# One sparse expert moved to the end of a mixture-of-experts stage, and two weight transfers moved ahead of the first gather

## Chip, cores, metric

One core of a Trainium2 chip runs the whole layer. The metric is device time in microseconds (us) from start to end of one execution; the figure quoted is the median over the runs. TensorE, VectorE, ScalarE, GpSimd and SyncE are called PE, DVE, ACT, POOL and SP, as in the profile.

## The reference

One layer on 512 tokens of width 1024, float32. A mixer (differential attention and a Mamba-2 scan, both projected from one matrix) adds to the residual, then a mixture of experts, then a gated per-layer embedding, then a norm. What matters here is the experts:

```
h = rms_norm(x)
logits = h @ router_w + router_b               # 512 x 32
top_vals, top_idx = top_k(logits, 4); gate = softmax(top_vals)
for each token and each of its 4 experts e:
    gu = h @ w_up[e] + b_up[e]                 # 1024 -> 2048
    g, u = min(gu[:1024], 7), clip(gu[1024:], -7, 7)
    y += gate * (((u + 1) * g * sigmoid(1.702 g)) @ w_down[e] + b_down[e])
x = x + y
```

There are 512 x 4 = 2048 rows of work for 32 experts, 64 each on average. The weights of one expert are 8 MiB (`w_up`) and 4 MiB (`w_down`).

## The kernel before

All engines run hand-written programs joined by semaphores. Until about 780 us they compute the mixer. From there on:

**Routing.** PE does the output projection tile by tile (`out_proj`, 4 tiles of 128 tokens), DVE adds it to the residual `xs` (`add_out`, L1745) and normalizes it (`normalize`, L1345), ACT writes the normalized rows to `h2_dram` (`store_h2`, L1103). PE turns each tile, ACT copies the turned tile to `h_tile` (two buffers, `evacuate`, L1105), and PE multiplies it with the router (`route`, L2324). `h_tile` lies in the bytes that the first pair of rows of `w_up` will hold, so SP may load that pair only when all four tiles are routed. DVE picks the top four (`choose`, L1721), clears the bias tiles (memset, L1754), ranks the tokens of each expert, and builds the slot tables. `slot_token` (L1826) says which token fills which slot of which expert. It waits for all of `h2_dram` (L1824). Then DVE sorts experts by size (L1828 to L1857) and writes their order to `control`; `rows_u` (L1868) closes the tables, with `tables_ready` at 3.

**Rounds.** Each expert is a round `b` of 96 slots (`CAP`), or of 64 (`PAIR`) if it is one of the `SMALLS` = 14 experts with the fewest tokens. Round 0, 1 and 2 are large, then 14 pairs of a small and a large round follow (`pair`, L2558), and the last round, 31, is always expert 31, with 96 slots. If any expert doesn't fit, `extra` is positive and all engines run `AGAIN` = 35 further rounds. In a round POOL gathers the tokens (`fetch`, L729), PE turns them (`turn_x`, L2413), DVE copies them to `x_T` (`copy_x`, L1873), PE multiplies with `w_up` (`up`, L2432, or `up_small`, L2453), ACT and DVE form the activation (`swish`, `take_u`, `join`), PE turns it (`turn_act`, L2421), ACT copies it (`copy_act`, L1165), and PE multiplies with `w_down` (`down`, `down_small`). PE's order is `up(b)`, `turn_x(b+1)`, `down(b-1)`, `turn_act(b)`. ACT stores the rows to `y_dram` (`expert_out`, L1144).

**Weights.** `w_up` and `w_down` have one buffer each, in four pairs of row blocks (2 MiB and 1 MiB per pair). SP loads pair `c` of the next expert when PE has used it: `up_used`, `down_used` (L555, L569). All matmuls carry L2026 and all transfers of `w_up` and `w_down` carry L556 and L570.

**End.** The last round's rows are not stored. `down_last` (L2526) leaves them in PSUM, and PE spreads them over the tokens with a 0/1 matrix (`hot_last`, L1891, `turn_last_slots`, `sum_last`). The other rows come from `y_dram` by 16 indirect gathers on POOL (`gather_rows`, L759), which DVE adds up (`gather`, L1937). Rows of the last round's expert in `y_dram` are zeroed early by a DMA on ACT's queue (L835).

The order of SP's queue around the routing, before:

```
load_up(0, 0, 1, 2)                    # pair 1 of expert 0
sp.wait_ge(out_projected, 2 * TT - 1)
load_up(0, 0, 2)                       # pairs 2 and 3
sp.wait_ge(routed, TT)
load_up(0, 0, 0, 1)                    # pair 0
for k in range(4): ...                 # w_pg_raw[k], 0.5 MiB each
...                                    # biases of expert 0
sp.wait_ge(xg_landed, 16)              # the first gather
load_down(0, 0)                        # pairs 0 to 3
```

Of the kernel before, what the change touches and what calls it, by code (L numbers as in the profile page):

```python
# [54 lines left out]
SMALLS, FIRST_SMALL, PAIR = 14, 3, 64  # L55
# [49 lines left out]
H_AT, ZERO_AT, MOE_AT, ARENA = 87, 127, 97, 131  # L105
# [49 lines left out]
def build(nc, x, p, mix_norm_w, w_in, lambda_q1, lambda_k1, lambda_q2, lambda_k2, da_head_norm_w,  # L155
# [3 lines left out]
    with ExitStack() as ctx:  # L159
# [43 lines left out]
        def h_tile_of(t):  # L203
            return h_tile[:, t % 2]

# [70 lines left out]
        h_tile, mix_w = at(4, 2, KT, P), at(H_AT, D)  # L276
# [108 lines left out]
        last_hot = at(MOE_AT + 13, TT * TOPK, CAP)  # L385
        last_slots = at(MOE_AT + 25, TT, CAP)
# [8 lines left out]
        y_hi = [y_hi_main[0:CAP, 0:512], y_hi_main[0:CAP, 512:WIDE], y_hi_side[0:CAP]]  # L395
        y_lo = [y_lo_main[0:CAP], y_lo_side[0][0:CAP], y_lo_side[1][0:CAP]]
# [89 lines left out]
        def _(sp):  # L486
# [79 lines left out]
            def load_down(i, expert):  # L566
                for c in range(KT // 2):
# [27 lines left out]
            load_down(0, 0)  # L595
# [17 lines left out]
            load_down(EXPERTS - 1, EXPERTS - 1)  # L613
            load_bias_down(EXPERTS - 1, EXPERTS - 1)
# [44 lines left out]
        def _(pool):  # L659
# [108 lines left out]
            pool.wait_ge(y_zeroed, 16 * (HEADS + 1))  # L768
            with pool.If(extra > 0):
                experts_again()  # L770
                pool.wait_ge(y_stored, 32 * (ROUNDS - 1))
                gather_rows(BLOCKS * CAP)
# [10 lines left out]
        def _(act):  # L783
# [50 lines left out]
            last_row = (EXPERTS - 1) * CAP  # L834
            act.dma_start(y_dram[last_row:last_row + PAIR], zero_rows[0:PAIR]).then_inc(y_zeroed, 16)  # L835
# [208 lines left out]
            act.wait_ge(y_zeroed, 16 * (HEADS + 1))  # L1044
# [42 lines left out]
            def root_out(t):  # L1087
                n = TT + t
                if t == 0:
                    root_mean(1, t, xs[:, t, :], lambda: act.wait_ge(x1_ready, 1), D, at(0, D))  # L1090
                    return
                act.wait_ge(x1_ready, 2 * t)
                own.then(act.activation(at(0, 512), xs[:, t, 0:512], ACT.Square, accum_out=first_half[:, t, 0:1]))
# [3 lines left out]
                own.then(act.activation(at(2, 512), xs[:, t, 512:D], ACT.Square, accum_out=stat[:, n, 0:1]))  # L1097
                act.activation(stat[:, n, 1:2], stat[:, n, 0:1], ACT.Sqrt, bias=first_half[:, t, 1:2], scale=1.0 / D
                               ).then_inc(norm_rooted, 1)
# [5 lines left out]
            def evacuate(t):  # L1105
                wait(act, routed, t - 1)
                turned = psum[:, 4 * 512:6 * 512].rearrange("p (k t) -> p k t", t=P)
                if t < TT - 1:
                    act.wait_ge(xn_turned, TT + t + 1)
                    act.activation(h_tile_of(t), turned, ACT.Copy).then_inc(h_ready, 1)  # L1110
                    return
                act.wait_ge(tail_turned, 1)
                act.activation(h_tile_of(t)[:, 0:TT], turned[:, 0:TT], ACT.Copy).then_inc(tail_copied, 1)
                act.wait_ge(xn_turned, TT + t + 1)
                act.activation(h_tile_of(t)[:, TT:KT], turned[:, TT:KT], ACT.Copy).then_inc(h_ready, 1)
# [54 lines left out]
            def copy_last_slots():  # L1170
                act.wait_ge(slots_summed, 2)
                act.activation(slots_last[0:CAP], psum[0:CAP, 3 * 512:4 * 512], ACT.Copy).then_inc(ple_copied, 1)

            def keep_last(b):

                act.wait_ge(down_done, b + 1)
                for cols, part, last in zip(LAST_COLS, y_hi, (True, False, True)):
                    ins = act.activation(part, psum[0:CAP, cols], ACT.Copy)
                    if last:
                        ins.then_inc(y_ready, 1)  # L1180

# [11 lines left out]
            swish(0)  # L1193
            copy_last_slots()
# [25 lines left out]
            swish(EXPERTS - 1)  # L1220
# [3 lines left out]
            copy_act(EXPERTS - 1)  # L1224
# [3 lines left out]
            with act.If(extra > 0):  # L1228
                for half in range(2):
                    ins = act.activation(y_kept[half][0:CAP], psum[0:CAP, half * 512:half * 512 + 512], ACT.Copy)  # L1230
# [7 lines left out]
                expert_out(ROUNDS - 1, 1)  # L1238

# [4 lines left out]
                for half in range(2):  # L1244
                    ins = act.activation(psum[0:CAP, half * 512:half * 512 + 512], y_kept[half][0:CAP], ACT.Copy)
# [77 lines left out]
        def _(dve):  # L1323
# [430 lines left out]
            dve.memset(arena[:, kb(MOE_AT + 28):kb(MOE_AT + 32)], 0.0)  # L1754
# [68 lines left out]
            for b in range(2):  # L1823
# [4 lines left out]
            sorted_of = slice(2, EXPERTS - 1)  # L1828
            own.mark(dve.tensor_tensor(inc, excl, full_total, ALU.add))
            key = [by_size[0:1, i, sorted_of] for i in range(3)]  # L1830
            own.then(dve.tensor_scalar(key[2], last[0:1, 0, sorted_of], -float(EXPERTS * P), SIZE_BASE, ALU.mult, ALU.add))
            own.then(dve.tensor_tensor(key[0], key[2], iota_far[0:1, sorted_of], ALU.add))
            own.then(dve.max(smallest[0:1, 0:8], key[0]))
            own.mark(dve.max_index(small_at[0:1, 0:8], smallest[0:1, 0:8], key[0]))
            own.then(dve.scalar_tensor_tensor(out=key[1], in0=key[0], scalar=smallest[0:1, 7:8], in1=key[0],
                                              op0=ALU.is_lt, op1=ALU.mult))
            own.then(dve.max(smallest[0:1, 8:16], key[1]))
# [6 lines left out]
            own.mark(dve.max_index(small_at[0:1, 8:16], smallest[0:1, 8:16], key[1]))  # L1844
            own.then(dve.scalar_tensor_tensor(out=key[2], in0=key[0], scalar=smallest[0:1, SMALLS - 1:SMALLS],
                                              in1=iota_far[0:1, sorted_of], op0=ALU.is_lt, op1=ALU.mult))
            own.mark(dve.tensor_copy(small_of[0:1], small_at[0:1]))
            own.then(dve.max(others[0:1, 0:8], key[2]))
            own.mark(dve.tensor_scalar(small_of[0:1], small_of[0:1], 2.0, None, ALU.add))
            own.then(dve.scalar_tensor_tensor(out=key[1], in0=key[2], scalar=others[0:1, 7:8], in1=key[2],  # L1850
                                              op0=ALU.is_lt, op1=ALU.mult))
            own.then(dve.max(others[0:1, 8:16], key[1]))
            own.then(dve.tensor_scalar(other_of[0:1], others[0:1], -1.0 / P, float(EXPERTS - 1), ALU.mult, ALU.add))
            dve.tensor_copy(control[:, 2:4 + 2 * SMALLS].rearrange("o (q c) -> o q c", c=2)[:, :, 0],
                            other_of[0:1, 0:SMALLS + 1])
            dve.tensor_copy(control[:, FIRST_SMALL:FIRST_SMALL + 2 * SMALLS].rearrange("o (q c) -> o q c", c=2)[:, :, 0],
                            small_of[0:1, 0:SMALLS])  # L1857
# [33 lines left out]
            def hot_last():  # L1891

                own.then(dve.tensor_scalar(row_f, row_f, float((EXPERTS - 1) * CAP), None, ALU.subtract))
                for n in range(TT * TOPK):
                    own.mark(dve.tensor_scalar(last_hot[:, n, :], iota_slot, row_f[:, n:n + 1], None, ALU.is_equal))
# [29 lines left out]
            take_u(EXPERTS - 1)  # L1925
            join(EXPERTS - 1)
# [18 lines left out]
            def split_last():  # L1945
                for i, (cols, hi, lo) in enumerate(zip(LAST_COLS, y_hi, y_lo)):
                    dve.wait_ge(y_ready, 2 * EXPERTS - (i == 0))
                    ins = dve.tensor_tensor(lo, psum[0:CAP, cols], hi.bitcast(F32), ALU.subtract)
# [75 lines left out]
        def _(pe):  # L2024
# [299 lines left out]
            def route(t):  # L2324
# [107 lines left out]
            def up(b, order=STRIP_ORDER):  # L2432
                pe.wait_ge(x_copied, b + 1)
                wait(pe, u_ready, b)
                for k in range(KT):
# [3 lines left out]
                    for r in range(STRIPS):  # L2439
                        for j in range(STRIPS):  # L2440
                            mm(bank(r)[strip(j)], x_T[:, k, strip(order[j])],
                               up_both[k][:, :, r * QUARTER:(r + 1) * QUARTER], k == 0, False)
                        ins = mm(bank(r)[strip(STRIPS)], x_T[:, k, strip(order[r])], up_both[k][:, :, WIDE:FF],
# [82 lines left out]
            def down_last(i):  # L2526
# [15 lines left out]
                for half in range(2):  # L2542
                    ins = mm(bank(half)[0:CAP], ones_bf[0:32, 0:CAP], bias_dn[0:32, half * 512:half * 512 + 512], False, True)
                ins.then_inc(down_done, 1)

            def turn_last_slots():
                pe.wait_ge(slots_ready, TT + 1)
                for t in range(TT):
                    ins = pe.transpose(psum[0:CAP, 3 * 512 + t * P:3 * 512 + (t + 1) * P], last_slots[:, t, :], ident[:])
# [13 lines left out]
            def experts(again):  # L2563
# [115 lines left out]
```

## Time and profile before

| | us |
|---|---|
| median of 3 runs | 1942.35 (1941.89 to 1944.38) |
| the profiled execution | 1940.7 |
| its span, first to last instruction | 1938.9 |

The mean granted TensorE clock of the profiled execution is 0.997. A chain row gives start, length and what the time went to. A landing time is from the issue of a transfer to its last byte. A wait for several semaphores is put down to the one that came last.

### The profile page before, as it was taken

The numbers are of one execution on the slowest core, as the hardware profiler recorded it, in microseconds if no ns is written. First come the engines' busy times: TensorE is split into PE (matmuls) and PEld (weight loads), VectorE is DVE, ScalarE is ACT, GpSimd is POOL, SyncE is SP. The second block draws the span as 40 slices with busy tenths as digits, with TensorE's granted clock in tenths as the row PEclk, the third lists the DMA queues.
The fourth block names the chain that finished last, engine by engine and source line by source line (L and its number), as shares of the span: only waits on it lengthen the run. The fifth ranks groups of instructions, "written<-read, shape, count | busy, mean of one in ns | idle before, by whom it ended". The sixth has DMA issues, their size and how long they took to land.

```text
span 1938.9 us, 34408 instructions
## 1 busy us (share of the span) xinstructions
PE 1831.4 (94%) x14020; PEld 1084.0 (56%) x14020; DVE 705.5 (36%) x1106; ACT 473.2 (24%) x729; POOL 102.8 (5%) x137
## 2 busy tenths in 40 slices
PE   6999999999999999989999988998899889989998
PEld 4777788888888888843343332433333333333346
DVE  5666768887765345361000000000000000000056
ACT  3444443525435243220110000101000000000036
POOL 2000001001020000000000000000000000000030
PEclk9999999999999999999999999999999999999999
DMA  4333322222222443279999999999999999999962
GB/s 131 88 87 102 94 76 66 66 65 65 65 66 66 118 143 109 112 316 408 400 421 425 422 425 423 424 423 423 424 422 422 421 424 416 420 422 421 387 228 105
DMA packets 171005, 510.85 MB, mean 263 GB/s; under 512 B 14293, under 2 KB 124838, under 8 KB 138118
## 3 DMA queue, kind: packets, MB, share of 16 engines
q1 hardware_dynamic: 154480, 474.67, 62.5%
q10 hardware_dynamic: 9494, 17.58, 2.7%
q0 software_dynamic: 6912, 16.79, 2.4%
q8 instruction: 102, 1.67, 0.4%
q14 instruction: 17, 0.14, 0.0%
HBM read 497.79 MB, written 19.60 MB: 267 GB/s over the span
## 4 chain that ended last, share of the span: by engine, by line
PE 77%; DMA 15%; DVE 4%; ACT 2%; issue 1%; ACTq 0%; DVEq 0%; POOL 0%; SPq 0%
PE psum L2026 73%; DMA arena<-in_w_up 15%; PE psum L2417 1%; PE psum L2426 1%; DVE arena L1445 1%; PE psum L2088 0%; PE psum L2196 0%; DMA arena<-y_dram,rows_u 0%; PE psum L2156 0%; ACT w_hi L817 0%; PE psum L2141 0%; DVE w_lo L1329 0%; DVE arena L1513 0%; DVE arena L1359 0%; DVE arena L1424 0%
## 5 line engine op out<-in xcount | busy, mean ns | idle before, releaser
L2026 PE MATMUL psum<-arena 128*32 128x512 f32 (+3 forms) x9344 | 981.9, 538 | 71.2 <-DMA arena<-in_w_up 58.9
L2026 PEld LDWEIGHTS psum<-arena 128*32 128x32 f32 (+2 forms) x9344 | 388.6, 116 | 613.7 <-issue 432.0
L1879 DVE TENSOR_SCALAR arena<-psum 128x768 f32<-128x768 f32 (+1 forms) x32 | 26.9, 841 | 906.9 <-ACT arena L1142 906.9
L2026 PE MATMUL psum<-h_hi,w_hi 128*128 128x512 f32 x640 | 258.7, 404 | 1.3 <-DVE w_lo L1329 1.3
L2026 PE MATMUL psum<-h_hi,w_lo 128*128 128x512 f32 x640 | 249.9, 390 | 0.0
L2026 PE MATMUL psum<-h_lo,w_hi 128*128 128x512 f32 x640 | 249.4, 390 | 0.0
L1329 DVE TENSOR_TENSOR w_lo<-arena,w_hi 128x1024 fp32r<-128x1024 f32 x104 | 135.6, 1305 | 187.7 <-ACT w_hi L817 186.7
L1142 ACT ACTIVATE arena<-psum 128x768 f32<-128x768 f32 (+1 forms) x32 | 22.9, 717 | 574.4 <-PE psum L2026 574.4
L2026 PEld LDWEIGHTS psum<-h_hi,w_hi 128*128 128x128 f32 x640 | 120.3, 188 | 33.9 <-issue 8.2
L2026 PEld LDWEIGHTS psum<-h_lo,w_hi 128*128 128x128 f32 x640 | 120.4, 188 | 26.4 <-issue 2.9
L2026 PEld LDWEIGHTS psum<-h_hi,w_lo 128*128 128x128 f32 x640 | 120.1, 188 | 25.9
L817 ACT ACTIVATE w_hi<-arena 128x1024 fp32r<-128x1024 f32 x104 | 109.6, 1055 | 96.1 <-PE psum L2026 96.1
L1168 ACT ACTIVATE arena<-psum 128x768 f32<-128x768 f32 (+1 forms) x32 | 22.9, 717 | 321.3 <-PE psum L2426 321.3
L743 POOL DMA_INDIRECT arena<-h_dram,block_token x30 | 30.6, 1021 | 573.6 <-PE psum L2417 573.6
L891 ACT ACTIVATE arena<-psum 128x512 f32<-128x512 f32 x40 | 23.8, 596 | 149.7 <-PE psum L2026 149.6
L709 POOL TENSOR_TENSOR arena<-after,gdta 128x1024 f32<-128x1024 f32 x16 | 33.0, 2063 | 509.7 <-DVE gdta L1528 369.6
L1513 DVE SCALAR_TENSOR_TENSOR arena<-arena,gconv 128x512 f32<-128x512 f32 x72 | 54.2, 752 | 2.5
L2026 PE MATMUL psum<-ys_hi,w_hi 128*128 128x512 f32 x128 | 49.8, 389 | 0.0
L2026 PE MATMUL psum<-ys_lo,w_hi 128*128 128x512 f32 x128 | 49.8, 389 | 0.0
L2026 PE MATMUL psum<-ys_hi,w_lo 128*128 128x512 f32 x128 | 49.8, 389 | 0.0
L871 ACT ACTIVATE arena<-arena,small 128x128 f32<-128x128 f32 (+3 forms) x64 | 35.5, 555 | 31.1 <-DVE small L1451 31.1
L2417 PEld LDWEIGHTS psum<-ident,arena 96*128 96x128 f32 x256 | 33.1, 214 | 11.4 <-issue 9.8
(383 smaller groups left out, 1623.1 us busy)
## 6 DMA issues: line engine op xcount, KB each, us to landing
arena<-in_w_up SPq DMA_DIRECT2D x128, 2048.0 KB, 25.7
arena<-in_w_down SPq DMA_DIRECT2D x128, 1024.0 KB, 26.0
arena<-in_w_in SPq DMA_DIRECT2D x80, 512.0 KB, 3.9
arena<-in_w_ssd_branch SPq DMA_DIRECT2D x16, 512.0 KB, 4.0
y_dram<-arena ACTq DMA_DIRECT2D x17, 288.0 KB, 7.1
y_dram<-arena ACTq DMA_DIRECT2D x8, 512.0 KB, 4.0
arena<-in_w_attn_branch SPq DMA_DIRECT2D x8, 512.0 KB, 3.9
arena<-in_w_out SPq DMA_DIRECT2D x8, 512.0 KB, 4.4
```

The source lines that it names most:

```text
L709: pool.tensor_tensor(dta_after, after[:].unsqueeze(1).broadcast_to([P, HG, P]), gdta[:, c, :].unsqueeze(2).broadcast_to([P, HG, P]), ALU.m ...
L743: pool.indirect_dma_start(xg, None, h2_dram, bass.IndirectOffsetOnAxis(token, 0), bounds_check=SEQ - 1, oob_is_err=False).then_inc(xg_land ...
L817: act.activation(w_hi[:, unit.slot], w_raw[unit.slot], ACT.Copy).then_inc(hi_ready, 1)
L871: ins = act.activation(s, s, ACT.Exp, bias=amax[:, 2 * q + m:2 * q + m + 1], accum_out=asum[:, 2 * q + m:2 * q + m + 1])
L891: act.activation(dst, bank(n % 2), ACT.Copy).then_inc(proj_copied, 1)
L1142: act.activation(g_sb[:, 0:n], up_psum[:, 0:n, 0, :], ACT.Silu, scale=ALPHA).then_inc(sig_ready, 1)
L1168: act.activation(act_T[:, 0:n], turned_act[:, 0:n], ACT.Copy, scale=1.0 / ALPHA).then_inc(act_copied, 1)
L1329: dve.tensor_tensor(w_lo[:, unit.slot], w_raw[unit.slot], w_hi[:, unit.slot].bitcast(F32), ALU.subtract).then_inc(lo_ready, 1)
L1513: ins = dve.scalar_tensor_tensor(out=o, in0=r[:, k:k + SEQ], scalar=gconv[:, k, i:i + 1], in1=o, op0=ALU.mult, op1=ALU.add)
L1879: dve.tensor_scalar(u_sb[:, 0:n], up_psum[:, 0:n, 1, :], 1.0 + LIMIT, 1.0 - LIMIT, ALU.min, ALU.max).then_inc(u_ready, 1)
L2026: return pe.matmul(o, l, r, start=start, stop=stop)
L2417: ins = pe.transpose(turned_x[:, k, :], xg[0:CAP, k // 2 * 2 * P + k % 2:(k // 2 + 1) * 2 * P:2], ident[0:CAP, 0:CAP])
```

## The change

Four things. The round that stays in PSUM becomes the smallest expert by tokens instead of expert 31, so the sort covers experts 2 to 31 with 15 small ones, the last round has 64 slots (`up_small`, four turned blocks instead of six, `down_last` with 64 tokens per matmul), and its rows of `y_dram`, no longer known in advance, are zeroed by two DMAs on ACT's queue after the tables are ready (`clear_last`), from a strip that DVE's memset of the bias tiles now also clears. `h_tile` becomes one buffer at another place and the square dumps of `root_out` move too, so pair 0 of `w_up` for expert 0 no longer waits for the router. SP's queue has a new order: pairs 0 and 1 of `w_up` first, then pairs 2 and 3 and the four parts of `w_ple_gate` after the output projection, then half of `w_down` for expert 0 after the router, and only its other half after the first gather. The sort's small operations run on 128 partitions instead of one, since every partition needs the last expert's first row (`last_row`).

```diff
-SMALLS, FIRST_SMALL, PAIR = 14, 3, 64
+SMALLS, FIRST_SMALL, PAIR = 15, 3, 64
+PAIRS = SMALLS - 1
...
-        h_tile, mix_w = at(4, 2, KT, P), at(H_AT, D)
+        h_tile, mix_w = at(OALL_AT, KT, P), at(H_AT, D)
...
-            load_up(0, 0, 1, 2)
+            load_up(0, 0, 0, 2)
             sp.wait_ge(out_projected, 2 * TT - 1)
             load_up(0, 0, 2)
-            sp.wait_ge(routed, TT)
-            load_up(0, 0, 0, 1)
             for k in range(4):
                 sp.dma_start(w_pg_raw[k], w_ple_gate[0, k * P:(k + 1) * P, :]).then_inc(w_pg_landed, 16)
+            sp.wait_ge(routed, TT)
+            load_down(0, 0, 0, 2)
...
             sp.wait_ge(xg_landed, 16)
-            load_down(0, 0)
+            load_down(0, 0, 2)
...
-            act.dma_start(y_dram[last_row:last_row + PAIR], zero_rows[0:PAIR]).then_inc(y_zeroed, 16)
...
             def evacuate(t):
-                wait(act, routed, t - 1)
+                wait(act, routed, t)
...
+            def clear_last():
+                at_block = act.value_load(control[0:1, EXPERTS - 1:EXPERTS], min_val=0, max_val=EXPERTS - 1)
+                for half in range(2):
+                    act.dma_start(y_dram[ds(at_block * CAP, PAIR), half * 512:half * 512 + 512], no_rows).then_inc(y_zeroed, 16)
...
             swish(0)
+            clear_last()
             copy_last_slots()
...
-            swish(EXPERTS - 1)
+            swish(EXPERTS - 1, small=True)
...
-            dve.memset(arena[:, kb(MOE_AT + 28):kb(MOE_AT + 32)], 0.0)
+            dve.memset(arena[:, kb(MOE_AT + 28):kb(ARENA)], 0.0)
...
-            sorted_of = slice(2, EXPERTS - 1)
+            sorted_of = slice(2, EXPERTS)
...
+            dve.tensor_copy(control[:, EXPERTS - 1:EXPERTS], small_of[0:1, 0:1])
+            own.mark(dve.tensor_scalar(last_row[:], small_of[:, 0:1], float(CAP), None, ALU.mult))
...
-                        if k < 2 * STRIPS:
-                            ins = mm(bank(half)[0:CAP], act_T[:, k, 0:CAP], w[:, cols], k == 0, False)
-                        else:
-                            for j in range(STRIPS):
-                                ins = mm(bank(half)[strip(j)], act_strip(k, j), w[:, cols], False, False)
+                        c = k // 2
+                        tokens = act_T[:, 2 * (c % 2) + k % 2, PAIR * (c // 2):PAIR * (c // 2 + 1)]
+                        ins = mm(bank(half)[0:PAIR], tokens, w[:, cols], k == 0, False)
...
-                up(EXPERTS - 1, range(STRIPS))
+                up_small(EXPERTS - 1)
                 down(EXPERTS - 2)
-                turn_act(EXPERTS - 1, last=True)
+                turn_act(EXPERTS - 1, last=True, small=True)
                 down_last(EXPERTS - 1)
```

## Rows read from the trace of the kernel before

**Rows 1.** Busy time by stretch; the last three columns are clock, DMA share, GB/s.
```profile
894.00:956.00 62.00, 62.00 (x694) 27.20 (x690) 5.38 (x6) 4.73 (x7) 2.59 (x5) 1.00 0.99 391
1212.46:1276.36 63.90, 58.20 (x589) 22.37 (x588) 4.84 (x6) 5.02 (x7) 2.40 (x4) 1.00 1.01 423
1770.00:1780.00 10.00, 7.74 (x56) 2.08 (x60) 0.00 (x0) 0.00 (x0) 0.00 (x0) 0.83 1.02 428
```

**Rows 2.** The chain that ended last, through the tables to the first round.
```profile
835.59 0.91 DVE arena L1754
...
851.40 0.21 DVE slot_token L1826
...
858.69 0.97 DVE arena L1873
859.70 21.23 PE psum L2026 x204
```

**Rows 3.** DVE in order of time, two copies to the control table.
```profile
854.67 0.17 DVE L1854 CAST control<-arena 1x15 int32<-1x15 f32 x1
854.75 0.15 DVE L1856 CAST control<-arena 1x14 int32<-1x14 f32 x1
```

**Rows 4.** SP's issues in order of time.
```profile
780.98 56.93 SPq L556 DMA_DIRECT2D arena<-in_w_up  x4
837.96 2.24 SPq L589 DMA_DIRECT2D pg_raw<-in_w_ple_gate  x4
...
865.12 15.78 SPq L556 DMA_DIRECT2D arena<-in_w_up  x4
```

**Rows 5.** Two windows of the `w_up` line, each with its issues and landing time.
```profile
L556 SPq DMA_DIRECT2D arena<-in_w_up x1: 341/341/341, 830.3 to 830.3; - x1
...
DMA to landing us min/median/max: 7.9/7.9/7.9
...
L556 SPq DMA_DIRECT2D arena<-in_w_up x2: 367/370/373, 892.7 to 897.9; - x2
...
DMA to landing us min/median/max: 7.9/8.0/8.1
```

**Rows 6.** Last store to h2_dram, landing times of all four, and of the first gather.
```profile
833.77 0.33 ACTq L1103 DMA_DIRECT2D h_dram<-arena  x1
...
DMA to landing us min/median/max: 2.6/2.6/10.5
...
DMA to landing us min/median/max: 3.6/3.6/3.6
```

**Rows 7.** Expert 31's `w_up`, then round 30's `w_down`: issues and landing times.
```profile
L556 SPq DMA_DIRECT2D arena<-in_w_up x4: 332/344/365, 1803.3 to 1818.9; - x4
...
DMA to landing us min/median/max: 24.0/24.1/24.3
...
L570 SPq DMA_DIRECT2D arena<-in_w_down x4: 332/344/362, 1822.1 to 1827.3; - x4
...
DMA to landing us min/median/max: 23.6/24.8/25.9
```

**Rows 8.** The chain that ended last, from a first small round to the end.
```profile
955.16 14.41 PE psum L2026 x136
...
981.54 0.68 PE psum L2426 x4
...
1118.31 26.06 DMA arena<-in_w_up
1144.41 4.18 PE psum L2026 x40
...
1797.86 21.09 PE psum L2026 x204
...
1828.32 31.92 PE psum L2026 x306
1860.24 0.93 PE psum L2426 x6
```

More of the change, by code:

```diff
@@ L564, in load_bias_up, with load_down @@
                                  rows[:, r:STRIPS + 1:STRIPS - r]).then_inc(bias_up_landed, 16)
-            def load_down(i, expert):
-                for c in range(KT // 2):
+            def load_down(i, expert, start=0, end=KT // 2):
+                for c in range(start, end):
                     if not isinstance(i, int) or i:
@@ L1096, in root_out @@
                 act.wait_ge(x1_ready, 2 * t + 1)
-                own.then(act.activation(at(2, 512), xs[:, t, 512:D], ACT.Square, accum_out=stat[:, n, 0:1]))
+                own.then(act.activation(at(DUMP_AT + 2, 512), xs[:, t, 512:D], ACT.Square, accum_out=stat[:, n, 0:1]))
                 act.activation(stat[:, n, 1:2], stat[:, n, 0:1], ACT.Sqrt, bias=first_half[:, t, 1:2], scale=1.0 / D
@@ L1223, in _ @@
                 split_gate(k)
-            copy_act(EXPERTS - 1)
+            copy_act(EXPERTS - 1, small=True)
             expert_out(EXPERTS - 2)
@@ L1229, in _ @@
                 for half in range(2):
-                    ins = act.activation(y_kept[half][0:CAP], psum[0:CAP, half * 512:half * 512 + 512], ACT.Copy)
+                    ins = act.activation(y_kept[half][0:PAIR], psum[0:PAIR, half * 512:half * 512 + 512], ACT.Copy)
                 ins.then_inc(ple_copied, 1)
@@ L1238, in _ @@
                 expert_out(ROUNDS - 1, 1)
+                act.wait_ge(y_stored, 32 * (ROUNDS - 1))
+                clear_last()
                 act.wait_ge(w_pg_landed, 32 * KT)
@@ L1244, in _ @@
                 for half in range(2):
-                    ins = act.activation(psum[0:CAP, half * 512:half * 512 + 512], y_kept[half][0:CAP], ACT.Copy)
+                    ins = act.activation(psum[0:PAIR, half * 512:half * 512 + 512], y_kept[half][0:PAIR], ACT.Copy)
                 ins.then_inc(ple_copied, 1)
@@ L1827, in _ @@
                               ).then_inc(tables_ready, 1)
-            sorted_of = slice(2, EXPERTS - 1)
+            sorted_of = slice(2, EXPERTS)
             own.mark(dve.tensor_tensor(inc, excl, full_total, ALU.add))
[L1830 to L1835, printed above, removed]
+            key = [by_size[:, i, sorted_of] for i in range(3)]
+            own.then(dve.tensor_scalar(key[2], last[:, 0, sorted_of], -float(EXPERTS * P), SIZE_BASE, ALU.mult, ALU.add))
+            own.then(dve.tensor_tensor(key[0], key[2], iota_far[:, sorted_of], ALU.add))
+            own.then(dve.max(smallest[:, 0:8], key[0]))
+            own.mark(dve.max_index(small_at[:, 0:8], smallest[:, 0:8], key[0]))
+            own.then(dve.scalar_tensor_tensor(out=key[1], in0=key[0], scalar=smallest[:, 7:8], in1=key[0],
                                               op0=ALU.is_lt, op1=ALU.mult))
-            own.then(dve.max(smallest[0:1, 8:16], key[1]))
+            own.then(dve.max(smallest[:, 8:16], key[1]))
             own.then(dve.scalar_tensor_tensor(out=owner[0:1, 31:32], in0=smallest[0:1, SMALLS - 1:SMALLS],
@@ L1841, in _ @@
             dve.tensor_copy(control[:, FLAG:FLAG + 1], owner[0:1, 31:32]).then_inc(tables_ready, 1)
[L1844 to L1848, printed above, removed]
@@ L1849, in _ @@
-            own.mark(dve.tensor_scalar(small_of[0:1], small_of[0:1], 2.0, None, ALU.add))
-            own.then(dve.scalar_tensor_tensor(out=key[1], in0=key[2], scalar=others[0:1, 7:8], in1=key[2],
+            own.mark(dve.max_index(small_at[:, 8:16], smallest[:, 8:16], key[1]))
+            own.then(dve.scalar_tensor_tensor(out=key[2], in0=key[0], scalar=smallest[:, SMALLS - 1:SMALLS],
+                                              in1=iota_far[:, sorted_of], op0=ALU.is_lt, op1=ALU.mult))
+            own.mark(dve.tensor_copy(small_of, small_at))
@@ L1924, in _ @@
                 turn_over(b + 1)
-            take_u(EXPERTS - 1)
-            join(EXPERTS - 1)
+            take_u(EXPERTS - 1, small=True)
+            join(EXPERTS - 1, small=True)
             for k in range(KT):
```

73 lines of the change are left out of this document (39 added, 34 removed).

## The prediction

> **What bounds the kernel now.** I read the busy time by stretch first. From about 860 us on the DMA engines never rest, but at two different rates. In a pair of rounds in the middle they move 423 GB/s while PE is busy 58.2 of 63.9 us: there the weights are the bound. Between 894 and 956 us PE is busy all 62 us and the DMA engines move 391 GB/s: there PE is the bound, and SP can only issue a transfer when PE has freed its buffer [rows 1]. The chain of waits agrees: from 859.70 us it stays on PE, and its first long piece of `w_up` transfer begins at 1118.31 us [rows 2, 8].
>
> The landing times say how much is queued. A pair of `w_up` issued at 830.3 us, onto an idle queue (SP's pair before it is that of 781 us), takes 7.9 us [rows 4, 5]. The two issued at 892.7 and 897.9 us take 8.1 and 7.9 us, so nothing was queued ahead of them either [rows 5]. At the end a pair takes 24 us [rows 7]. So the queue that makes the later rounds DMA-bound is built after 898 us, and what lies ahead of it has been worked off by then.
>
> The end was read last. Expert 31's `w_up` was issued from 1803.3 to 1818.9 us, evenly, 5.2 us apart; with 24.3 to 24.0 us each the pairs land at 1827.6, 1832.5, 1837.9 and 1843.0 us [rows 7]. PE starts that product at 1828.32 us and a large one takes 21.09 us, about 5.2 us per pair, so it needs the pairs at 1828.3, 1833.5, 1838.7 and 1843.8 us [rows 8]. It runs within 1 us behind the data all the way. Then `down(30)` takes the rest of the 31.92 us, and the chain goes through the store, POOL's gathers and the embedding gate. That tail moves as a block.
>
> **The change, part by part.**
>
> *The early transfers.* Pair 0 of `w_up` goes from 837.6 us to 781 us, and half of `w_down` (2.1 MB) goes from behind the first gather to where that pair was. So 2.1 MB less are to be moved after 856 us, which is 2.1 / 0.423 = 5.0 us of DMA time [rows 1, 4]. The question is whether that reaches the end. PE waits for no weight in the first rounds, so landing earlier gives it nothing. SP's next issues are tied to PE: pair 0 of expert 1 at 865.12 us, a pair's time after PE's start at 859.70 us, and so on [rows 2, 4]. With an empty queue at 892.7 us already, the 5.0 us turn into idle DMA time before 893 us. I take 0. The other end is 5.0 us, if the slowest of the 16 engines has in truth not rested since 860 us; the equal landing times (7.9 and 7.9 to 8.1 us) are the row nearest to this and speak for 0.
>
> *DVE's work ahead of the first round.* The memset grows from 4 to 6 KiB per partition: 0.91 us becomes 1.37 us, so +0.46 us, and it is on the chain [rows 2]. After the sort one copy and one multiplication are new. Two such copies start 0.08 us apart [rows 3], and the multiplication likewise, so +0.17 us with rounding up. The sort itself costs DVE by row length, 30 columns instead of 29, and the number of partitions is not in its duration: the write of `slot_token`, 96 partitions of 53 columns, takes 0.21 us and a copy of 15 columns on one partition 0.17 us, so 0 [rows 2, 3]. `copy_x(0)` at 858.69 us follows the tables directly, and PE follows it: +0.63 us. Later all rounds are paced by PE's start, then by a DMA queue that PE's issues fed, so this stays to the end. If DMA had slack instead, it would be 0.
>
> *`h_tile` in one buffer, the dumps elsewhere.* `evacuate(t)` now waits for the router's product of tile t-1. PE issues that product before it turns tile t, which `evacuate` waits for anyway. Hidden by PE's own order: 0. Without that cover it would cost a router product per tile: 8 matmuls of 32 columns, where a step of 512 columns takes 14.41 / 16 = 0.9 us [rows 8], so far less than 7 us.
>
> *`clear_last` and the hot rows.* The two DMAs stand on ACT's queue behind `swish(0)`, ahead of two copies that wait for PE; 0.25 MB is 0.6 us of DMA time, in the stretch where the engines now have 5.0 us to spare. 0, at most 0.6 us. `hot_last` gets shorter under `up(0)`: 0.
>
> *The last round at 64 slots.* `up_small` costs 14.41 us where `up` costs 21.09 us [rows 8], so 6.68 us if only PE counted. But the data land no earlier. A small product takes 3.6 us per pair (14.41 less the biases, by four). On the clock of before: pair 0 at 1828.3, done 1831.9; pair 1 lands 1832.5, done 1836.1; pair 2 lands 1837.9, done 1841.5; pair 3 lands 1843.0, and from there a small round takes 4.18 us to its end [rows 8]: 1847.3 us with 0.1 us for the start. Before it was 1828.32 + 21.09 = 1849.4 us. So 2.1 us, not 6.7. Then `down(30)` needs 2.6 us per pair, and its pairs land at 1822.1 + 23.6 = 1845.7 to 1827.3 + 25.9 = 1853.2 us [rows 7]; started at 1847.3 us it wants the last one at 1855.1 us. No new wait. Bounds: 6.7 us if the data come early, 0.4 us if PE's clock drops behind the three new waits as it did after those before 1780 us (clock 0.83 over 10 us, 1.7 us lost) [rows 1].
>
> *The turn behind it.* `turn_act(31)` has 4 blocks instead of 6, 0.68 for 0.93 us [rows 8]: -0.25 us, ahead of the store on ACT. `down_last` streams the same 512 columns 16 times, with 64 instead of 96 tokens held: 0.
>
> *Sum.* +0.63 - 2.1 - 0.25 = -1.7 us. The profiled execution would take 1940.7 - 1.7 = 1939.0 us (span 1937.2). The median of the runs is 1.65 us above that execution, so the forecast is 1942.35 - 1.7 = 1940.6 us.
>
> **A rule against the change.** The last store to `h2_dram` was issued at 833.77 us, behind two pairs of `w_up`, and took 10.5 us; the others took 2.6 us. It landed at 844.3 us, and DVE writes `slot_token`, which needs it, at 851.40 us [rows 2, 6]. So ACT's transfer waited for SP's. Now 2.1 MB of `w_ple_gate` also stand ahead: 849.3 us, 2 us early. The Trainium skill (DMA: Bandwidth & Descriptors, "Issuing engines are not separate DMA queues") says that transfers of SP, ACT and POOL share the same 16 engines, so more of SP's ahead of the store is no free ride; by that the trace agrees. The same page's section "Queues, rings and completion order" says the engines take turns between the queues' rings packet by packet; by that the store would hardly feel the added load, and 10.5 against 2.6 us doesn't look like it. By either the sum is unchanged; only the rival below loses or gains.
>
> **The rivals.**
>
> *The early bytes do reach the end.* Then a queue that never ran dry also hides DVE's delay, and it is -5.0 instead of +0.63 us: -7.35 us, 1935.0 us. For: the DMA share is 0.99 to 1.0 everywhere behind 860 us. Against: 391 GB/s and the landing times. A part of it is possible: every 1 us of queue that was left at 893 us is 1 us won.
>
> *The last round isn't held by its data.* Then 6.7 instead of 2.1 us: -6.3 us, 1936.0 us. It needs the last pair 4.5 us earlier in relation to PE, which nothing moves. If the first rival is true, PE and data move together, and this doesn't come on top.
>
> *The store or the gather is late: slower.* If half of `w_down`, issued around 837.6 us, also gets ahead of the store, it lands at 854.3 us, 2.9 us behind `slot_token`'s time, and all tables follow: +2.9 + 0.17 - 2.35 = +0.7 us, 1943.1 us. If the gather (3.6 us before) queues behind that half too, up to 5.0 us more, of which about 1 us is covered by DVE's tables: +4.7 us, 1947.1 us. It decides from a landing of the store at 853.6 us on. Against: the bytes asked for between 830 and 850 us are the same in sum, 8.9 MB with the store.
>
> *A fifteenth small expert doesn't fit.* Then `extra` is positive and 36 more rounds of about 32 us run, some 1,150 us. The profile can't show this. I counted the reference's router on its inputs: of experts 2 to 31 the fifteenth smallest has 61 tokens, and 64 fit.
>
> **Chances and range.** The sum 64 in 100; the early bytes reach the end, mostly or in part, 14; the last round not held 9; the late store or gather 8; the rest (a little more or less in start or tail) 5, of which 1 for the extra rounds. About 0.2% (3.9 us) is what this kernel's measurement can tell from no change. Faster by more than that: 14 + 9 + 1 = 0.24. Slower: the upper part of the late store and the rest, 0.08. Within: 0.68. The range takes in both early rivals nearly whole and the lower part of the late store: 1935.5 to 1943.6 us. The likeliest case alone has 1939.0 to 1942.3 us.
>
> **What would show it.** The memset at 1.37 us and PE's first round at about 860.3 us. A landing time of expert 1's last pair some 5 us shorter than before, then 7.9 again at 893 us with a dip in GB/s before it: that is the lost 5.0 us. If instead the rounds behind 1118 us run about 5 us earlier, the first rival is right. In the last `up_small`, three waits for `w_up` of about 0.6, 1.8 and 1.5 us, and its end 19 us after its start. `h2_dram`'s last landing near 849 us. The forecast is wrong if the waits in the last round are missing, or if PE's start is later than 861 us.

## The result, and the profile after

| us | before | after |
|---|---|---|
| median | 1942.76 (1941.04 to 1946.01, 12 runs) | 1947.39 (1942.2 to 1948.1, 12 runs) |
| ratio to before, 95% interval | | 1.0016 [1.0009, 1.0024] |
| profiled execution | 1940.7 | 1945.91 |
| its span | 1938.9 | 1943.8 |
| its mean granted clock | 0.997 | 0.989 |

The kernel became slower, by 4.6 us between the medians and by 3.1 us (1.7 to 4.7) by the ratio. The forecast was 1940.6 us in a range up to 1943.6 us. Lines moved with the edit: PE's matmuls are L2037 after, `turn_act` L2437, the memset L1762, `copy_x` L1883, `add_last` (the addition behind `sum_last`) L1966, `ple_turn` L2620.

The granted clock tells the two traces apart first. The views by stretch of after: start, length, busy us of PE, PEld, DVE, ACT, POOL, then granted clock, DMA share, GB/s.

```profile
850.00:860.00 10.00, 4.81 (x23) 2.53 (x22) 8.32 (x47) 1.38 (x3) 1.81 (x2) 0.91 0.64 236
860.00:870.00 10.00, 9.03 (x68) 2.43 (x72) 7.18 (x22) 1.09 (x1) 0.61 (x2) 0.75 1.05 418
892.00:894.00 2.00, 2.00 (x24) 0.65 (x20) 0.00 (x0) 0.00 (x0) 0.00 (x0) 0.94 0.53 205
894.00:896.00 2.00, 2.00 (x24) 0.57 (x20) 0.00 (x0) 0.00 (x0) 0.18 (x1) 1.00 0.04 11
894.00:956.00 62.00, 62.00 (x686) 26.68 (x682) 5.38 (x6) 3.93 (x5) 2.41 (x4) 1.00 0.94 367
1875.00:1895.00 20.00, 18.25 (x59) 13.49 (x58) 17.33 (x17) 5.90 (x10) 12.62 (x11) 0.66 0.84 294
1880.00:1892.00 12.00, 11.63 (x37) 9.30 (x36) 9.51 (x9) 3.75 (x5) 7.17 (x7) 0.50 0.91 353
```

The same stretches of before:

```profile
850.00:860.00 10.00, 6.20 (x22) 3.12 (x26) 8.22 (x43) 2.48 (x3) 2.24 (x2) 0.83 0.69 254
860.00:870.00 10.00, 10.00 (x96) 2.99 (x92) 7.58 (x20) 0.00 (x0) 0.18 (x1) 1.00 1.00 417
1875.00:1895.00 20.00, 17.25 (x92) 13.08 (x87) 17.97 (x19) 7.43 (x13) 13.68 (x12) 1.00 0.86 305
```

A mean of 0.50 over a whole stretch is the lower of the two levels, 1.2 instead of 2.4 GHz. Between 1880 and 1892 us PE ran at it throughout, and PE was busy 11.63 of these 12 us. At the start, before has its low part in 850 to 860 us, and after has most of it in 860 to 870 us, where PE's first round already runs. The row 894 to 896 us is the hole in the transfers: 11 GB/s.

The chain of waits of after, at the places that answer to [rows 2, 8]: start, length, what.

```profile
836.29 1.34 DVE arena L1762
...
859.96 0.97 DVE arena L1883
860.97 23.18 PE psum L2037 x204
...
888.84 22.79 PE psum L2037 x204
...
924.50 21.09 PE psum L2037 x204
...
1064.10 19.87 DMA arena<-in_w_up
...
1146.77 4.18 PE psum L2037 x40
...
1799.95 20.78 PE psum L2037 x192
...
1887.47 10.06 PE psum L2037 x33
...
1907.30 0.88 PE psum L2620 x8
...
1919.07 0.87 PE psum L2620 x8
```

And the pieces of before's chain that answer to these and weren't needed until now:

```profile
885.91 22.41 PE psum L2026 x204
...
921.20 3.98 PE psum L2026 x33
...
1877.45 0.69 DVE y_lo_main L1948
...
1884.88 7.81 PE psum L2026 x33
...
1902.41 0.87 PE psum L2611 x8
...
1914.19 0.87 PE psum L2611 x8
```

Set side by side, the shift of after against before, in us:

| at | before | after | shift |
|---|---|---|---|
| `copy_x(0)` | 858.69 | 859.96 | +1.27 |
| `up(2)` | 921.20 | 924.50 | +3.30 |
| a round that waits for its weights | 1144.41 | 1146.77 | +2.36 |
| start of `up_small(31)`, before `up(31)` | 1828.32 | 1830.34 | +2.02 |
| end of `down(30)` | 1860.24 | 1860.51 | +0.27 |
| the split of the last rows | 1877.45 | 1877.38 | -0.07 |
| the third `ple_turn` | 1902.41 | 1907.30 | +4.89 |

Up to `up(2)` the shift grows because `up(0)` and `up(1)` together take 45.97 instead of 43.64 us. Then the weights become the bound (after waits for `w_up` from 1064 us on already, before from 1118 us), and it shrinks. Behind the split, 33 matmuls that took 7.81 us take 10.06 us, and the +4.9 us stay to the end.

So in these two profiles the start lost 2.0 us (0.6 us of it in the mixer, whose code is the same in both), the last round with its turn and its last product won 2.1 us, and all that is left arises after 1877 us.

The last round, PE's instructions in order of time, idle time in brackets:

```profile
1830.34 3.64 PE L2037 MATMUL psum<-arena 128*32 128x512 f32 x32
1835.16 3.64 PE L2037 MATMUL psum<-arena 128*32 128x512 f32 x32 [1.18 <-DMA arena<-in_w_up]
1840.43 3.64 PE L2037 MATMUL psum<-arena 128*32 128x512 f32 x32 [1.63 <-DMA arena<-in_w_up]
1845.49 3.64 PE L2037 MATMUL psum<-arena 128*32 128x512 f32 x32 [1.43 <-DMA arena<-in_w_up]
```

There stand the three waits that were forecast.

Last, the groups that keep shapes apart: the sums over the last round's slots (`sum_last`) before, PE between 1877 and 1884 us, with busy us, mean ns, then idle time.

```profile
L2026 PE MATMUL psum<-y_lo_side,slots_last 96*128 96x256 f32 x8 | 2.2, 294 | 0.0
L2026 PE MATMUL psum<-y_hi_main,slots_last 96*128 96x512 f32 x4 | 1.8, 444 | 1.2 <-ACT y_hi_side L1178 1.2
```

The same after, between 1877 and 1887 us:

```profile
L2037 PE MATMUL psum<-y_lo_side,slots_last 64*128 64x256 f32 x8 | 3.5, 433 | 0.2 <-DVE y_lo_side L1959 0.2
L2037 PE MATMUL psum<-y_hi_main,slots_last 64*128 64x512 f32 x4 | 2.5, 635 | 1.2 <-ACT y_hi_side L1178 1.2
```

The count and the columns are the same. What the edit changed is the number of rows over which they contract, 64 instead of 96 (the first figure of 64*128). The longer time, 433 for 294 ns, is the clock's and not the shape's. The first sums of each kernel, before the clock fell in after, and one from the middle, in the order before, after, before, after:

```profile
1877.95 0.62 PE L2026 MATMUL psum<-y_hi_main,slots_last 96*128 96x512 f32 x2 [1.23 <-ACT y_hi_side L1178]
1877.58 0.61 PE L2037 MATMUL psum<-y_hi_main,slots_last 64*128 64x512 f32 x2 [1.22 <-ACT y_hi_side L1178]
...
1880.02 0.28 PE L2026 MATMUL psum<-y_hi_side,slots_last 96*128 96x256 f32 x1
1880.87 0.41 PE L2037 MATMUL psum<-y_hi_side,slots_last 64*128 64x256 f32 x1
```

At full clock 64 rows take as long as 96 (0.61 and 0.62 us), and at the lower level 96 rows take the same 0.41 us too (e5 below, at 1880.97 us). The 64 rows follow from the 64 slots of the last round, and they stand in no step of the forecast.

### The profile page after: what moved, and what is told of

The parts are those of the page before. It is cut to its first block, busy times and chain, and to the rows that moved or that the text cites. A ratio compares the mean times of both kernels' runs of the same rounds, so it can differ in the third digit from the quotient of the medians.

```text
span 1943.8 us, 34263 instructions
## 1 busy us (share of the span) xinstructions
PE 1831.2 (94%) x13934; PEld 1084.4 (56%) x13934; DVE 703.9 (36%) x1108; ACT 472.8 (24%) x729; POOL 102.5 (5%) x137
## 4 chain that ended last, share of the span: by engine, by line
PE 75%; DMA 17%; DVE 4%; ACT 2%; issue 1%; ACTq 0%; DVEq 0%; POOL 0%; SPq 0%
PE psum L2037 71%; DMA arena<-in_w_up 17%; PE psum L2428 1%; PE psum L2437 1%; DVE arena L1453 1%; PE psum L2099 0%; PE psum L2207 0%; PE psum L2167 0%; ACT w_hi L819 0%; PE psum L2152 0%; DMA arena<-y_dram,rows_u 0%; DVE w_lo L1337 0%; DVE arena L1521 0%; DVE arena L1367 0%; DVE arena L1432 0%
## 5 line engine op out<-in xcount | busy, mean ns | idle before, releaser
L2037 PE MATMUL psum<-arena 128*32 128x512 f32 (+4 forms) x9264 | 977.7, 538 | 75.0 <-DMA arena<-in_w_up 63.2
L2037 PEld LDWEIGHTS psum<-arena 128*32 128x32 f32 (+2 forms) x9264 | 385.9, 116 | 615.7 <-issue 426.1
L2037 PE MATMUL psum<-h_hi,w_hi 128*128 128x512 f32 x640 | 258.7, 404 | 1.3 <-DVE w_lo L1337 1.3
L2037 PE MATMUL psum<-h_hi,w_lo 128*128 128x512 f32 x640 | 249.9, 390 | 0.0
L2037 PE MATMUL psum<-h_lo,w_hi 128*128 128x512 f32 x640 | 249.4, 390 | 0.0
L2037 PEld LDWEIGHTS psum<-h_hi,w_hi 128*128 128x128 f32 x640 | 120.3, 188 | 34.4 <-issue 8.7
L2037 PEld LDWEIGHTS psum<-h_lo,w_hi 128*128 128x128 f32 x640 | 120.4, 188 | 26.4 <-issue 2.9
L2037 PEld LDWEIGHTS psum<-h_hi,w_lo 128*128 128x128 f32 x640 | 120.1, 188 | 25.8
L2037 PE MATMUL psum<-ys_hi,w_hi 128*128 128x512 f32 x128 | 49.8, 389 | 0.0
L2037 PE MATMUL psum<-ys_lo,w_hi 128*128 128x512 f32 x128 | 49.8, 389 | 0.0
L2037 PE MATMUL psum<-ys_hi,w_lo 128*128 128x512 f32 x128 | 49.8, 389 | 0.0
L2428 PE MATMUL psum<-ident,arena 96*128 96x96 f32 x256 | 38.4, 293 | 2.2 <-DMA arena<-h_dram,slot_token 2.2
```

What stands on the lines that cost most here:

```text
L2037: return pe.matmul(o, l, r, start=start, stop=stop)
L2428: ins = pe.transpose(turned_x[:, k, :], xg[0:CAP, k // 2 * 2 * P + k % 2:(k // 2 + 1) * 2 * P:2], ident[0:CAP, 0:CAP])
```

## The experiments

Each kernel was timed in 5 rounds against before on the same chip. "Tail" is the granted clock in the profiled execution between 1875 and 1895 us, `up(0)` and `up(1)` the lengths in its chain.

| kernel | median (lowest to highest) | ratio [95%] | `up(0)`, `up(1)` | tail |
|---|---|---|---|---|
| e1_wide_last | 1945.82 (1944.46 to 1948.93) | 1.0014 [1.0005, 1.0023] | 24.16, 21.09 | 0.74 |
| e2_narrow_before | 1942.42 (1941.12 to 1945.47) | 0.9996 [0.9987, 1.0005] | 21.23, 22.27 | 0.91 |
| e3_last_only | 1946.15 (1941.26 to 1947.99) | 1.0011 [1.0002, 1.002] | 23.28, 22.79 | 0.74 |
| e4_transfers_only | 1943.45 (1941.56 to 1945.3) | 1.0000 [0.9991, 1.0009] | 22.93, 21.09 | 1.00 |
| e5_sum96 | 1942.56 (1940.84 to 1946.44) | 1.0002 [0.9993, 1.0011] | 23.22, 22.79 | 0.91 |
| e6_sum64_before | 1945.04 (1942.65 to 1947.43) | 1.0010 [1.0001, 1.0019] | 21.23, 22.24 | 0.66 |
| e7_sum96_wide | 1943.49 (1941.67 to 1944.97) | 1.0002 [0.9993, 1.0011] | 23.18, 22.78 | 0.91 |
| e8_sum128 | 1942.97 (1939.17 to 1948.38) | 1.0001 [0.9992, 1.0011] | 22.92, 21.09 | 1.00 |
| e9_pool_clears | 1940.89 (1938.68 to 1945.17) | 0.9990 [0.9981, 0.9999] | 23.75, 22.79 | 0.83 |
| e10_memset_before | 1945.19 (1943.36 to 1947.98) | 1.0011 [1.0002, 1.002] | 22.92, 21.09 | 1.00 |
| e11_after_again | 1946.78 (1943.56 to 1950.46) | 1.0019 [1.001, 1.0028] | 23.30, 22.79 | 0.74 |
| e12_no_transfers | 1942.51 (1939.78 to 1947.19) | 1.0002 [0.9993, 1.0011] | 21.23, 22.43 | 0.91 |

Before had medians of 1943.34 us beside e1 to e4, 1943.22 us beside e5 to e8, and 1942.92 us beside e9 to e12.

### Which part loses, and is it the width of the last product?

The first suspicion (A in the expectations) was `down_last`, which now works on 64 tokens' columns instead of 96. e1 gives after its old width back:

```diff
-tokens = act_T[:, 2 * (c % 2) + k % 2, PAIR * (c // 2):PAIR * (c // 2 + 1)]
-ins = mm(bank(half)[0:PAIR], tokens, w[:, cols], k == 0, False)
+at_col = P * (2 * (c % 2) + k % 2) + PAIR * (c // 2)
+tokens = act_T.rearrange("p k t -> p (k t)")[:, at_col:at_col + CAP]
+ins = mm(bank(half)[0:CAP], tokens, w[:, cols], k == 0, False)
...
```

> The changed kernel, but down_last holds 96 columns of act_T per matmul instead of 64 (the 32 behind them are stale and land in rows that nobody reads), so the number and length of PE's matmuls stay. Theory A: the changed kernel is late because PE's granted clock is 0.5 for 13.7 us from about 1879 us on, and what differs ahead of that is the 64-column down_last; then the drop is gone here and the time falls by about 5 us, to 1942 or less. Rival B: the drop comes from the new waits in the last up_small or from when the stages happen to fall; then it stays in most executions and the time stays at 1946 to 1948 us.

e2 narrows it in before. Through the order in which the strips of slots lie (0, 2, 1), the columns left out hold slots 32 to 63, which are filled: 14 of expert 31's 46 tokens get whatever stood in these rows of PSUM in place of its contribution. The expectation's words on empty slots don't hold; the matmuls' shapes are those intended.

```diff
-ins = mm(bank(half)[0:CAP], act_T[:, k, 0:CAP], w[:, cols], k == 0, False)
+ins = mm(bank(half)[0:PAIR], act_T[:, k, 0:PAIR], w[:, cols], k == 0, False)
...
-for j in range(STRIPS):
+for j in range(2):
...
```

> The kernel before, but down_last holds 64 columns instead of 96 (slots 64 to 95 of expert 31 are left out; it has 46 tokens, so these hold none). Theory A: the tail's clock drop appears and the time rises by about 5 us to 1947 or 1948 us. Rival B: no drop, 1942 to 1943 us.

e3 is after with SP's order, `h_tile` and the dumps of before, so what is left of the change is the last round, with DVE's added work for it; e4 is the reverse, before with these three moved.

```diff
-load_up(0, 0, 0, 2)
+load_up(0, 0, 1, 2)
 sp.wait_ge(out_projected, 2 * TT - 1)
 load_up(0, 0, 2)
+sp.wait_ge(routed, TT)
+load_up(0, 0, 0, 1)
 for k in range(4): ...
-sp.wait_ge(routed, TT)
-load_down(0, 0, 0, 2)
...
-load_down(0, 0, 2)
+load_down(0, 0)
...
```

> The changed kernel with SP's order around the routing, h_tile and the square dumps as before; only the small last round is left of the change. Theory A (all loss sits in the last round's clock): 1947 us, the same as the changed kernel. Rival C (the transfers lose time at the start, by an idle DMA queue or a late gather): 1943 to 1945 us.

> The kernel before with only SP's new order, the single h_tile and the moved dumps. My recorded step says 0: 1942 to 1943 us, DMA idle about 5 us before 893 us. Rival of the record (early bytes reach the end): 1935 to 1938 us. Rival C (the transfers lose time): 1944 to 1946 us.

e1 stays at 1.0014 and e2 at 0.9996: the width isn't the cause. (`down_last` also differs in its number of products: before does the last quarter of it in strips of 32 tokens, 48 matmul records in all against 32 after. e6 below keeps these strips and loses even so.) e3 carries the loss (1.0011) and e4 has none (1.0000). The view by stretch of e4 shows the hole behind 890 us and a tail at full clock:

```profile
888.00:898.00 10.00, 10.00 (x97) 3.12 (x100) 0.00 (x0) 0.81 (x1) 0.18 (x1) 1.00 0.71 267
1875.00:1895.00 20.00, 17.21 (x94) 12.64 (x89) 18.69 (x18) 6.62 (x11) 13.35 (x12) 1.00 0.86 306
```

267 GB/s where before has 406 GB/s in that stretch, and the time is the same: the bytes moved earlier become idle DMA time.

### The rows of the sums

With A gone, the shapes in the tail left one difference (D): `sum_last` contracts over 64 rows. e5 is after with 96, rows 64 to 95 of the 0/1 matrix being zero:

```diff
-tokens = slots_last[0:PAIR, t * P:(t + 1) * P]
+tokens = slots_last[0:CAP, t * P:(t + 1) * P]
...
+own.mark(act.activation(slots_last[PAIR:CAP], no_rows[0:CAP - PAIR], ACT.Copy))
...
-ins = act.activation(part, psum[0:PAIR, cols], ACT.Copy)
+ins = act.activation(part, psum[0:CAP, cols], ACT.Copy)
...
-ins = dve.tensor_tensor(lo, psum[0:PAIR, cols], hi.bitcast(F32), ALU.subtract)
+ins = dve.tensor_tensor(lo, psum[0:CAP, cols], hi.bitcast(F32), ALU.subtract)
```

> The changed kernel, but the products that spread the last round over the tokens (sum_last) contract over 96 rows as before the change instead of 64; rows 64 to 95 of the 0/1 matrix are zero, so the result is the same, and number and columns of the matmuls stay. Theory D: the tail's clock drop starts in these products since they use 64 instead of 96 rows of the array; then it is gone and the time falls to 1941 to 1943 us. Rival E (the whole tail sits on the edge, with 64 columns in down_last and 64 rows in the sums each adding): the drop stays in part of the executions, 1944 to 1946 us. Rival B (width and rows don't matter): 1946 to 1948 us.

e6 is the converse on before. It leaves out 14 tokens' rows of expert 31 in the sum, and nothing else.

```diff
-tokens = slots_last[0:CAP, t * P:(t + 1) * P]
+tokens = slots_last[0:PAIR, t * P:(t + 1) * P]
...
-ins = mm(psum[:, b + cols.start:b + cols.stop], tokens, (y_hi, y_lo)[i][n], i == 0, i == 1)
+ins = mm(psum[:, b + cols.start:b + cols.stop], tokens, (y_hi, y_lo)[i][n][0:PAIR], i == 0, i == 1)
```

> The kernel before, with sum_last contracting over 64 rows instead of 96 (rows 64 to 95, which hold 14 of expert 31's 46 tokens, are left out). Theory D: the clock falls to its lower level behind 1879 us in most executions, 1946 to 1948 us. Rivals B and E: little or no drop, 1943 to 1944 us.

The stretch of the tail in e5, and one shape of its sums between 1877 and 1884 us:

```profile
1875.00:1895.00 20.00, 17.29 (x80) 13.26 (x79) 18.45 (x18) 6.04 (x10) 14.58 (x12) 0.91 0.89 308
...
L2038 PE MATMUL psum<-y_lo_side,slots_last 96*128 96x256 f32 x6 | 2.3, 389 | 0.1
```

The same two of e6:

```profile
1875.00:1895.00 20.00, 18.33 (x67) 13.33 (x62) 16.37 (x17) 5.43 (x9) 12.10 (x11) 0.66 0.80 280
...
L2026 PE MATMUL psum<-y_lo_side,slots_last 64*128 64x256 f32 x6 | 2.6, 433 | 0.1
```

Padding with zeros, which computes nothing new, takes the low part (the time at the lower level between 1875 and 1895 us) from 13.7 us in after (clock 0.66) to 3.4 us (0.91) and the ratio from 1.0016 to 1.0002. Taking 32 rows away from before, with all transfers, waits and counts left alone, gives 13.7 us at the lower level, and 1.0010. Both directions agree, so the rows of the sums are shown as the cause of the tail's loss. The other runs bear it out: averaged over the 11 or 12 executions of each kernel, the mean granted clock is 0.990 to 0.992 with 64 rows in the sums (after, e1, e3, e6, e11) and 0.993 to 0.995 with 96 or 128 (before, e2, e4, e5, e7 to e10, e12).

Its size is less certain. e6 costs 1.8 us by medians, less than the 1946 us or more expected, and 2 us by its ratio (0.2 to 3.7 us). e5 saves 4.2 us against after in e11 by medians, which is another chip's, and 2.7 to 3.3 us by the ratios to before. The mean granted clock of e6's runs lies between 0.989 and 0.995, so its profiled execution (0.989) is one of the worse: the stretch isn't equally long in all of them.

The rows alone don't decide whether the clock falls, though. In stretches of 0.1 us, e5 is at the lower level from 1879.2 to 1882.7 us and after from 1878.7 to 1892.4 us. Either falls 1.1 us after its first sum. With 96 rows the clock was back while the sums still ran; with 64 rows it stayed low through all of them and for 5 us of the 128-row products behind them. What the rows changed between these two is how long the low stretch lasts; between before and e6, whether there is one as well.

e7 has both 96-row sums and e1's wide `down_last`; e8 is e5 with all 128 rows (`P` for `CAP` in each line).

```diff
-ins = mm(bank(half)[0:PAIR], tokens, w[:, cols], k == 0, False)
+ins = mm(bank(half)[0:CAP], tokens, w[:, cols], k == 0, False)
...
```

> The changed kernel with both: 96 columns in down_last and 96 rows in sum_last. Theory D: as with 96 rows alone, 1941 to 1943 us. Theory E: only this one is free of the drop, 1941 to 1943 us, while the 96 rows alone are 2 us or more above it. Rival B: 1946 to 1948 us.

```diff
-tokens = slots_last[0:CAP, t * P:(t + 1) * P]
+tokens = slots_last[0:P, t * P:(t + 1) * P]
...
```

> The changed kernel with all 128 rows in sum_last (rows 64 to 127 of the 0/1 matrix zero). Theory D: no drop, 1941 to 1943 us, and if more rows help further, less time at the lower clock than with 96. Rival B: 1946 to 1948 us.

Neither is told from e5 (1.0002, 1.0001, 1.0002). e8's profile has the tail at 1.00, but the times don't show it. 96 rows are enough.

### DVE's added work

With the tail mended, e5 still isn't faster than before, though the last round wins 2 us. The other loss is at the start. If DVE's 0.63 us moves `up(0)` into a low stretch of the clock (F), it costs more than its length. e9 is e5 with DVE's additions gone but for one small copy: POOL clears the strip while DVE ranks, and `last_row` is worked out behind the tables.

```diff
-dve.memset(arena[:, kb(MOE_AT + 28):kb(ARENA)], 0.0)
+dve.memset(arena[:, kb(MOE_AT + 28):kb(MOE_AT + 32)], 0.0)
...
+pool.wait_ge(out_projected, 2 * TT - 1)
+pool.memset(no_rows, 0.0).then_inc(consts_ready, 1)
...
-own.mark(dve.tensor_scalar(last_row[:], small_of[:, 0:1], float(CAP), None, ALU.mult))
```

> The changed kernel with 96 rows in the sums, and DVE relieved ahead of the first round: the strip of zeros is cleared by POOL, DVE's memset has its old size, and the multiplication for the last expert's first row comes after the tables. Theory F: DVE's longer work delays PE's first round by 0.6 us and in the profiled executions also pushes PE's idle time so that the clock's lower level reaches into the first round (23.2 us instead of 21.2 us); then the first round starts 0.5 us earlier, the first two `up` rows sum to 43.6 to 44.0 us instead of 46.0 us in most executions, and the median falls by 1 to 2 us below the 96-row version's, to 1940.5 to 1941.5 us. Rival G: where the clock falls around the first rounds is chance, not tied to DVE's work; then it falls by 0.5 us at most, 1942 us or more.

e10 is before with only the longer memset and two more small copies:

```diff
-dve.memset(arena[:, kb(MOE_AT + 28):kb(MOE_AT + 32)], 0.0)
+dve.memset(arena[:, kb(MOE_AT + 28):kb(ARENA)], 0.0)
...
+for spare in range(29, 31):
+    dve.tensor_copy(owner[0:1, spare:spare + 1], small_of[0:1, 0:1])
```

> The kernel before with only DVE's added work: the memset of 6 KiB instead of 4, and two more small copies behind the sort. Theory F: 1 to 2.5 us slower, 1944 to 1945.5 us. Rival G: 0.6 us slower, 1943.5 to 1944 us.

e11 is after unchanged, beside them. e12 is e9 with SP's order, `h_tile` and dumps of before (the diff of e3).

> The changed kernel once more, as the comparison on this chip. Theory D with its tail drop: 1946 to 1948 us, and the granted clock low for about 10 to 14 us from 1879 us on. If it comes out at 1943 us here, the loss was a matter of the chip.

> As the version in which POOL clears the strip, but with SP's old order, two router tiles and the old dumps. My recorded step (the early transfers are worth nothing) and the run of the transfers alone say: the same as with them, within 0.5 us. Rival: they cost or give 1 us or more once the rest is in place.

The view by stretch of e10, around PE's first round:

```profile
860.00:870.00 10.00, 7.76 (x60) 2.21 (x64) 8.89 (x23) 1.28 (x1) 1.00 (x1) 0.83 0.98 399
```

e10 costs 2.3 us by medians (1.0011, so 0.4 to 3.9 us) for 0.63 us of DVE work, and e9 is 2.0 us faster than before on its chip where e5 is 0.7 us faster. So the added work costs 1.4 to 2.3 us by medians. That is more than its length, but neither pair alone excludes 0.63 us: it lies in e10's interval, and the intervals of e5 and e9 overlap.

That the surplus comes through the clock (F) isn't shown, and one run speaks against it. In e10's profile `up(0)` takes 22.92 instead of 21.23 us and `up(1)` 21.09 instead of 22.41 us, so the low stretch has changed its place, and the sum has grown by only 0.37 us. e4, without any added DVE work, has the same two lengths (22.93 and 21.09 us) and costs nothing (1.0000). In e9's profile, which is its slowest run (1945.17 us), the two take 46.54 us where F expected 43.6 to 44.0. What turns 0.63 us into more stays open.

e9, at 1940.89 us, is the fastest of all, and the only one faster than before with its whole interval (0.9990 [0.9981, 0.9999]). e12 lacks the early transfers and is 1.6 us slower than e9, but the two intervals overlap, so whether the transfers give something once the rest is mended stays open; the expected 0.5 us at most was not confirmed either.

## Why the prediction was wrong

**The tail: the step that failed.** "That tail moves as a block", and `down_last` at 0 with it. `down_last` itself was right: it took 13.95 us after and 14.10 us before. But the tail wasn't a block. The 64 slots reach on into `sum_last`, and from the first tile's sums on PE's granted clock was at its lower level for 13.7 us: 4.9 us in the profile. e5 takes most of the loss back, and e6 brings about some 2 us of it in before. The forecast went by columns and counts, thought of the clock only for the waits in the last round, and had no term for the sums. With the 4.9 us of the profile this step alone moves the forecast to 1945.5 us, out of the range; with the 2.7 to 3.3 us of the ratios it comes to 1943.3 to 1943.9 us, at the range's upper end.

**DVE's work: a term of the right length, and probably the wrong price.** +0.46 us for the memset was 0.43 us (1.34 less 0.91), and `copy_x(0)` was late by 0.69 us beyond what the mixer's end was already late (0.58 us; in its first 60 us that execution's clock was 0.89 against 1.00). Its effect was taken as +0.63 us and measured at 1.4 to 2.3 us (e10 +2.3 us, e9 against e5 -1.4 us, each taken against before beside it), with intervals that reach down to 0.63 us. The two steps together, some 3 us and some 1.5 us more, are about the 4.8 us between 1.7 us faster and 3.1 us slower. The prediction named a start later than 861 us as what would make it wrong; PE started at 860.97 us.

**The last round: right.** Waits of 1.18, 1.63 and 1.43 us against 0.6, 1.8 and 1.5 us, 19.3 us from PE's start to the end of the product and its biases against 19.0 us, and 1.75 us won against 2.1 us. The turn won 0.24 us for 0.25 us. That the last product is held by its data, and 6.7 us are not to be had, was right too.

**The early transfers: right.** 0 was taken, with "a dip in GB/s" before 893 us as the sign. The dip came at 892 to 896 us (205, then 11 GB/s), with PE 3 us later, and expert 1's last pair took 10.5 instead of 15.4 us. e4 measures 1.0000 [0.9991, 1.0009]. The rival of -7.35 us is refuted.

**The store to `h2_dram`: right in the sum, wrong in the reading.** I expected its landing near 849 us, behind 2.1 MB more. The DMA issues between 830 and 900 us of after say:

```profile
h_dram<-arena ACTq DMA_DIRECT2D x1, 512.0 KB, 10.6
```

10.6 us against 10.5 us, issued at 834.36 us: it landed at 845.0 us. The four parts of `w_ple_gate` were issued ahead of it, from 831.75 us on, and didn't delay it. The Trainium skill (DMA: Bandwidth & Descriptors, "Queues, rings and completion order") has the engines take turns between queues by packet. By that rule more bytes in SP's queue don't delay the store, and this trace agrees; the serial reading, which the prediction preferred, does not fit. The late store and late gather, rivals on the slow side, didn't come about (gather 3.5 us). The slow side came from elsewhere.

## What to carry to other kernels

A smaller shape can be dearer by what comes with it, so when a tile shrinks, follow it through every matmul that uses it and look at the granted clock there, not at counts and durations alone. Where a clock stays low through a run of short matmuls of few rows, try padding them with zero rows: here 32 zero rows cost nothing and gave back some 3 us. When the start of a matmul stream moves by half a microsecond, price it with a run: here it cost 1.4 to 2.3 us by medians. And don't price a low stretch by its place in one profile: e4 and e10 show the same one in `up(0)`, and only e10 is slower.

## What the runs showed of the hardware

**The clock fell while PE was busy.** In after PE was busy 11.63 of the 12 us from 1880 to 1892 us at a granted clock of 0.50. What it had done before the fall at 1878.7 us: `down_last`'s biases, a wait of 1.22 us, then three 64-row sums from 1877.58 us. With 96 rows the low part was 3.4 us (e5, e7, e12) or 6.8 us (e9), with 128 rows none (e8); in before and its variants with 96 rows, none (before, e4, e10) or 3.4 us (e2). With 64 rows it was 10.2 us (e1, e3, e11) or 13.7 us (after, e6), so the two groups don't overlap in any of the 14 profiles. The Trainium skill (TensorE: Matmul & The Clock Gate, "Part 1: The HAM clock gate") ties the two levels to how busy PE has been. The levels agree with this trace; how busy PE was doesn't by itself explain why the clock stayed low for 12 us of which PE was busy 11.63. The fall isn't bound to 64 rows: it is there in five of the eight profiles with 96 rows, only shorter. Why rows change its length isn't settled.

**The low stretches move between executions of one kernel.** After itself had 13.7 us of it in the tail in one profile and 10.2 us in the other (e11), and the mean clock of its 12 runs lies between 0.989 and 0.995, with times from 1942.2 to 1948.1 us. One profile of a kernel can't price such a stretch; e9's was its slowest run. At the start of the rounds the place of the low stretch went with the edits: the four kernels with neither the early transfers nor the added DVE work (before, e2, e6, e12) have `up(0)` at 21.23 us, and all ten others have it at 22.92 to 24.16 us. Yet e4, one of the ten, takes as long as before.
